# Neighbourhood heads first, the latent queries' and keys' units laid among them

## What is computed

```python
p = h @ w_in
q_lat, kv_lat, k_rope, na_qkv = split(p)
q = rmsnorm((rmsnorm(q_lat, q_norm) @ w_q_up).reshape(B, L, 8, 96), q_gain)
ckv = rmsnorm(kv_lat, kv_norm)
k_nope, v = split((ckv @ w_kv_up).reshape(B, L, 8, 128), [64])
k = rmsnorm(concatenate([k_nope, k_rope]), k_gain)
nq, nk = rmsnorm(na_q, na_q_gain), rmsnorm(na_k, na_k_gain)      # 8 neighbourhood (NA) heads of 64
```

## Time and profile before

| | us |
|---|---|
| median of 3 runs | 1404.86 (1399.4 to 1412.47) |
| the profiled execution's own time | 1393.2 |
| its span | 1391.4 |
| TensorE busy in the span | 1243.8 (89%) |
| VectorE busy | 605.8 (44%) |
| ScalarE busy | 272.8 (20%) |
| GpSimd busy | 201.1 (14%) |

### The profile page before, as it was taken

How to read it: one execution, slowest core, us unless ns; L and a number is a source line. 1 busy time by engine, 2 the same in 40 slices (tenths; PEclk the granted TensorE clock), 3 DMA queues, 4 the chain that set the end, 5 groups by cost and what they waited for, 6 DMA issues and landing times.

```text
span 1391.4 us, 26446 instructions
## 1 busy us (share of the span) xinstructions
PE 1243.8 (89%) x9235; PEld 720.8 (52%) x9236; DVE 605.8 (44%) x1303; ACT 272.8 (20%) x672; POOL 201.1 (14%) x249
## 2 busy tenths in 40 slices
PE   4899759989977899999989999999995989999996
PEld 3544435555454555555556565344545544555553
DVE  0221543435244244444454433578644243445445
ACT  1111323323020111121223212221001111222111
POOL 1021240000010022222210000111001022221231
PEclk9899968989977999999999999999995999999998
DMA  9542177776253199999993131100028059996794
GB/s 316 197 170 81 48 254 272 246 259 226 82 230 133 45 411 402 380 419 384 394 343 127 70 92 60 61 0 0 1 82 362 1 233 419 411 389 271 295 420 175
DMA packets 80145, 304.79 MB, mean 219 GB/s; under 512 B 10872, under 2 KB 11809, under 8 KB 54729
## 3 DMA queue, kind: packets, MB, share of 16 engines
q1 hardware_dynamic: 77098, 298.66, 55.5%
q10 hardware_dynamic: 2752, 4.53, 0.9%
q0 software_dynamic: 224, 0.61, 0.1%
HBM read 301.52 MB, written 2.24 MB: 218 GB/s over the span
## 4 chain that ended last, share of the span: by engine, by line
PE 83%; DVE 9%; issue 3%; DMA 1%; SPq 1%; ACT 1%; POOL 1%; POOLq 0%; DVEq 0%; ACTq 0%
PE banks L427 80%; DVE arena L949 4%; DMA arena<-in_ada_b 1%; DVE arena L1085 1%; PE banks L591 1%; SPq L1816 1%; ACT arena L1541 1%; POOL arena L1717 1%; PE banks L478 1%; DVE arena L1172 0%; DVE arena L1095 0%; SPq L1814 0%; PE banks L790 0%; DVE arena L1083 0%; DVE arena L960 0%
## 5 line engine op out<-in xcount | busy, mean ns | idle before, releaser
L427 PE MATMUL banks<-arena 32*128 32x256 f32 (+12 forms) x8904 | 1196.7, 425 | 78.0 <-DVE arena L949 15.6
L427 PEld LDWEIGHTS banks<-arena 128*32 128x32 f32 (+5 forms) x8904 | 679.3, 157 | 559.5 <-issue 405.5
L949 DVE TENSOR_TENSOR arena<-banks,arena 128x64 f32<-128x64 f32 (+4 forms) x284 | 113.9, 413 | 104.1 <-PE banks L427 69.7
L949 DVE TENSOR_TENSOR arena<-arena 128x384 f32<-128x384 f32 (+11 forms) x229 | 156.5, 689 | 4.5
L1205 DVE SCALAR_TENSOR_TENSOR arena<-arena 128x768 f32<-128x768 f32 x81 | 83.0, 1024 | 92.7 <-issue 88.5
L1742 POOL COPY arena<-arena 128x256 f32 x79 | 64.9, 822 | 289.3 <-PE banks L427 154.1
L1578 ACT ACTIVATE arena<-banks 128x512 f32<-128x512 f32 x79 | 47.2, 597 | 249.5 <-PE banks L427 249.5
L1215 DVE TENSOR_SCALAR arena<-arena 128x64 f32<-128x64 f32 x79 | 15.4, 195 | 174.9 <-ACT arena L1582 174.9
L1733 POOL TENSOR_TENSOR arena<-arena 128x256 f32<-128x256 f32 x81 | 59.6, 736 | 220.8 <-PE banks L427 220.8
L1716 POOL TENSOR_SCALAR arena<-arena 128x8 f32<-128x8 f32 (+2 forms) x28 | 10.4, 370 | 423.8 <-ACT arena L1438 297.6
L1304 DVE TENSOR_SCALAR arena<-arena 128x385 f32<-128x385 f32 x24 | 11.5, 481 | 82.4 <-ACT arena L1639 82.4
(11 more groups left out here) (144 smaller groups left out, 453.7 us busy)
## 6 DMA issues: line engine op xcount, KB each, us to landing
arena<-in_moe_w_gate SPq DMA_DIRECT2D x64, 1024.0 KB, 8.3
arena<-in_moe_w_up SPq DMA_DIRECT2D x64, 1024.0 KB, 10.4
arena<-in_moe_w_down SPq DMA_DIRECT2D x64, 1024.0 KB, 10.3
arena<-in_ada_w SPq DMA_DIRECT2D x24, 2048.0 KB
arena<-in_hy_w_in SPq DMA_DIRECT2D x6, 2048.0 KB
arena<-in_attn_w_in SPq DMA_DIRECT2D x3, 2048.0 KB
arena<-mod_rows SPq DMA_DIRECT2D x8, 512.0 KB, 10.2
arena<-in_attn_w_out SPq DMA_DIRECT2D x2, 2048.0 KB
```

The lines of the kernel that those rows point to most:

```text
L427: return pe.matmul(out, lhsT, rhs, start=start, stop=stop, skip_group_check=True)
L949: return dve.tensor_tensor(o, p, q, op)
```

## The change

The latent units go out of the block ahead of the heads; only the six NA units stay there. The heads' order is NA first. The seven latent units, in the order q 0, k 0 to k 3, q 1, q 2, are laid among the first 28 passes: unit b is produced in pass 4b, squared in 4b+1, reduced and raised to its power in 4b+2, normalised, turned and copied in 4b+3. The reduction and the normalising stand at the head of VectorE's pass. All 20 chunks are laid behind heads, one every 2.35 passes. The up-projection weights leave the ring and lie in room of their own (in the place of hT and of the gate rows), loaded behind chunk (0,6) and after the last NA value projection; the gate rows are loaded later. The bias is masked after the sixth power. PSUM banks are named: units 0 and 1, scores 2 and 3, transposed probabilities 4 and 5, head outputs 6, chunks and their columns 7.

```diff
+        wq = [v(HTO, NH * QK), v(HTO + NH * QK, NH * QK), v(MODO + 4 * D, NH * QK)]
+        wkv = v(MODO + 4 * D + NH * QK, NH * 2 * NOPE)
-        items0 = ([("ada", 0, n) for n in range(4)] + [("win", i) for i in range(4)] + [("up",)]
+        items0 = ([("ada", 0, n) for n in range(4)] + [("win", i) for i in range(4)]
...
-                 + [("q", t) for t in range(3)] + [("k", t) for t in range(4)])
+                 + [("q", 0)] + [("k", t) for t in range(4)] + [("q", 1), ("q", 2)])
...
-        at_unit = {7: chunks[0], 9: chunks[1]}
-        at_head = {int(2.6 * n) + 1: c for n, c in enumerate(chunks[2:])}
+        at_head = {int(2.35 * n) + 1: c for n, c in enumerate(chunks)}
-        heads = [(kind, t, hd) for kind in range(2) for t in range(T) for hd in range(NH)]
+        heads = [(kind, t, hd) for kind in (1, 0) for t in range(T) for hd in range(NH)]
+        def unit_stage(i, c):
+            b = (i - c) // 4
+            return 6 + b if (i - c) % 4 == 0 and 0 <= b < len(units) - 6 else None
...
@@ TensorE, produce and the heads
+                    pe.wait_ge(up_loaded, 64)
                     sig("latT").at(pe, t)
-                            o = open_(pe, "proj", i, [("normed", n)])
+                            o = open_(pe, "proj", i, [("normed", n)], j)
...
+                    if kind == 0 and hd == 0:
+                        sig("uT").at(pe, max(uT["q", t, 1], uT["k", 0 if t == 0 else 3, 1]))
-                    o = open_(pe, "S", i, [("expd", i)])
+                    o = open_(pe, "S", i, [("expd", i)], 2 + i % 2)
-                    o = open_(pe, "PT", i, [("PT", i)])
+                    o = open_(pe, "PT", i, [("PT", i)], 4 + i % 2)
-                        open_(pe, "O", i // 2, [("OT", i // 2)])
+                        open_(pe, "O", i // 2, [("OT", i // 2)], 6)
...
                     if i >= 2:
                         values(i - 2)
+                    if unit_stage(i, 0):
+                        produce(*units[unit_stage(i, 0)])
+                    if unit_stage(i, 3):
+                        turn_unit(*units[unit_stage(i, 3)])
                     if i in at_head:
-                        ada(*at_head[i])
+                        ada(*at_head[i], 7)
@@ VectorE (reduced and normalised are the two halves of the old unit loop)
+                for n in range(6):
+                    reduced(n)
+                    normalised(n)
                 for i in range(NU + 2):
+                    if unit_stage(i, 2):
+                        reduced(unit_stage(i, 2))
+                    if unit_stage(i, 3):
+                        normalised(unit_stage(i, 3))
                     if 1 <= i <= NU:
@@ ScalarE, behind the exponential
+                    if unit_stage(i, 1):
+                        square_unit(unit_stage(i, 1))
+                    if unit_stage(i, 3):
+                        turned(*units[unit_stage(i, 3)])
                     if i >= 2 and i % 2 == 1:
@@ GpSimd
+                for n in range(6):
+                    unit_power(n)
                 pool.wait_ge(in_bias, 16)
...
+                for n in range(6, len(units)):
+                    unit_power(n)
@@ SyncE
-                load(items0[8])
                 sp.dma_start(bias.rearrange("p a b c d -> p (a b c d)"), a["bias"]).then_inc(in_bias, 16)
-                for k in items0[9:]:
+                for k in items0[8:]:
                     load(k)
+                    if k == ("ada", 0, 6):
+                        sig("psum_proj").at(sp, proj["nv", T - 1, 0])
+                        for c in range(3):
+                            sp.dma_start(wq[c], a["mla_w_q_up"][0, c * P:(c + 1) * P, :]).then_inc(up_loaded, 16)
+                        sp.dma_start(wkv, a["mla_w_kv_up"][0]).then_inc(up_loaded, 16)
...
-                        if items[n][1:] == (0, 5):
+                        if items[n][1:] == (1, 5):
+                            sig("psum_proj").at(sp, proj["q", 2, 1])
                             load_gate(0, 0)
```

More of the change, by code:

```diff
@@ L285, in build @@
         number = {k: n for n, k in enumerate(items)}
-        ndma = {"ada": 2, "up": 2, "w3": 3}
+        ndma = {"ada": 2, "w3": 3}
         loads = [0, 0, 0]
@@ L337, in build @@
         n = 0
-        for kind, t in units + [("ck", 3)]:
+        for kind, t in units[:6] + [("ck", 3)] + units[6:]:
             for j in range(2 if kind in "qk" else 1):
@@ L557, in attention @@
                 produce("nq", 0)
[L558 to L565, removed]
-                        produce(*units[n + 1])
-                    if n in at_unit:
-                        ada(*at_unit[n])
+                for n, (kind, t) in enumerate(units[:6]):
+                    if n < 5:
+                        produce(*units[n + 1])
+                    else:
+                        for tt in range(T):
+                            produce("nv", tt)
+                        pe.wait_ge(in_ctx, 48)
+                        for tt in range(4):
+                            turn_latents(tt)
                     turn_unit(kind, t)
@@ L1019, in attention, with reduced @@
                     sig("lat").by(dve.tensor_copy(lat[:, t, QR + KVR:WIN0], kv[:, KVR:KVR + ROPE]), t)
[L1020 to L1023, removed]
+                def reduced(n):
+                    kind, t = units[n]
                     b = n % 2
@@ L1032, in attention, with normalised @@
                     sig("hms").by(red, n)
+                def normalised(n):
+                    kind, t = units[n]
+                    b = n % 2
                     sig("hrs").at(dve, n)
@@ L1044, in attention @@
                         sig("normed").by(tt(dv, dv, bc(nqg if kind == "nq" else nkg, NH, 1), ALU.mult), n)
-                        continue
+                        return
                     dv = d.rearrange("p (h w) -> p h w", h=NH)
@@ L1504, in attention @@
                 square_unit(0)
[L1505 to L1515 removed]
+                for n, (kind, t) in enumerate(units[:6]):
+                    if n < 5:
+                        square_unit(n + 1)
+                    else:
+                        for tt_ in range(T):
+                            o = read(act, "proj", proj["nv", tt_, 0])
+                            sig("nv").by(act.activation(V[:, tt_, NAW:], o, ACT.Copy), tt_)
+                        for tt_ in range(4):
+                            o = read(act, "latT", tt_).rearrange("p (c t) -> p c t", c=4)
+                            c0 = 0 if tt_ < T else 3
+                            sig("latT").by(act.activation(LT[:, c0:4, tt_ * P:(tt_ + 1) * P], o[:, c0:4, :], ACT.Copy), tt_)
                     turned(kind, t)
@@ L1780, in _, with unit_power @@
                     power(lat_rs[:, t, 0:2], lat_ms[:, t, 0:2], 2, "lat_rs", t)
-                for n in range(len(units)):
+                def unit_power(n):
                     sig("hms").at(pool, n)
                     power(hrs[:, n % 2, :], hms[:, n % 2, :], 8, "hrs", n)
+                for n in range(6):
+                    unit_power(n)
                 pool.wait_ge(in_bias, 16)
```

26 lines of the change are left out of this document (5 added, 21 removed).

## The result

The changed kernel takes 1417.73 us (median of 9, 1411.81 to 1420.24) against 1399.12 us of the kernel before, now a median of 9 (1394.26 to 1412.47). The ratio is 1.0135, 95% interval 1.0104 to 1.0165: 1.35% slower. The forecast was 0.7% slower and the range held the time. The forecast time, 1414.4 us, looks closer than it was: it was laid on a median of 1404.86, and the longer series moved that median down to 1399.12. The difference is 18.6 us, twice the 9.5 of the forecast and close to the +19.3 of the rival "the clock falls among the latent-tile heads". Of all runs in this document only three of units_mixed fell in a slower state of the chip; its median and ratio are given without them.

The account below looks back on a forecast made before the run. Heads were taken as chains filled by VectorE and ScalarE. Mark 47: 155.1 + 153.1 + 4.3 + 45.2 + 4 = 361.7 against 352.2, 9.5 us later; laid on the median, 1414.4 us, range 1404 to 1425, with rivals 1396 to 1430.

Parts of the forecast that it names:

- the clock falls among the latent-tile heads: Rival, 20%: sixteen heads and seven chunks at the lower clock, 13.8 us less the 4 charged; +19.3 us, 1424.
- The masking: Before the heads: masking the bias beside the value projections costs nothing and gains 5.4 us of contention.
- The stall: Before the first latent query: TensorE waits about 8.5 us for up-projection weights landing at 148.5, plus 2 us at lower clock.
- The units among the heads: Among the heads: seven latent units add 45.2 us, or 6.5 us each, what a unit costs alone.
- second rival: The rival "the clock stays up".
- a normalising: On VectorE ahead of the next reciprocal, all that follows waits: 20.5 us for seven, from 13 to 24.
- Reducing, 0.95 us in an idle of 0.74: 0.2 each: In head passes on VectorE: each unit's reduction mostly fits the wait for ScalarE's exponential; 1.4 us in all.
- The clock: Inside the heads: about five normalising pauses of TensorE lower the granted clock; 4 us charged (0 to 14).
- Turning the order of the two head kinds changes none of the 48 passes: Between marks 0 and 47: neighbourhood heads first costs nothing, so the old 153.1 us stay.
- The units hide: Rival, 15%: the heads have more room, so the 20.5 us of normalising go under waits; -11 us, 1394.
- the clock stays up: Rival, 12%: denser work gives back about 11 us the old heads lost to the clock; -7.5 us, 1397.
- no stall: Rival, 13%: weights arrive before TensorE asks, or the standing time is used; -1 us, 1404.

Follow-up runs that it names:

- units_mixed: Kernel before with early masking, weights loaded behind the bias, chunks behind seven units, and head pairs alternating between tiles: 1387.94 us, ratio 0.9929.
- fill_early: up_early with extra, unread matmuls in the passes with a normalising: 1386.41 us, ratio 0.9901 to the kernel before.
- mask_early: Kernel before with only the bias masking moved, after the sixth power instead of the last: 1390.14 us, ratio 0.9938.
- up_early: Changed kernel with up-projection weights loaded behind the bias and latent units ordered q 0 to q 2, k 0 to k 3: 1405.03 us, ratio 1.0106.
- fill_both: Changed kernel with extra, unread matmuls in the wait for the weights and in passes with a normalising: 1407.56 us, ratio 1.0059.
- fill_gaps: Changed kernel with extra, unread matmuls only in passes with a normalising, none in the wait for the weights: 1400.13 us, ratio 1.0009.
- na_first: mask_early with the neighbourhood heads first, all units still ahead of the heads: 1393.14 us, ratio 0.9997 to the kernel before.

## Why the prediction was right, and where it was short

**What bounds it.** Right. The heads had no room. With stall and pauses taken out (fill_early), the interleaved order reaches mark 47 at 211.7 us from the transposes and the separate one (mask_early) at 209.9.

**The masking.** Right, with its cover. The last unit's products take 5.4 us less in mask_early, and mark 0 comes 6.0 us earlier. In the changed kernel the collision stands at 118.06, where a product takes 3.15 us, and TensorE does not wait for it.

**The stall.** The mechanism was right, the cold start was right, and the size was 2 us short. Landing was predicted for 148.5 and came at 149.0, but that agreement is luck: the chunk's load was predicted to be issued at 136.26 and was issued at 134.81, so the weights took 14.2 us and not 12.2. TensorE asked 4.0 us behind the start of the transposes (138.6 and 134.62), as predicted (140 and 136.06). So it stood 10.4 us and not 8.5. For the lower clock behind the stall 2 us were added, and 2.2 were measured. From the transposes mark 0 was predicted at 19.0 us and came at 21.4. up_early confirms the price by taking it away: 12.7 us at mark 0.

**The units among the heads.** 45.2 us were predicted. What fill_both leaves for them, 202.2 - 153.1 - 4.3 = 44.8 us, looks like a confirmation and is none. The 153.1 us of the old heads contain about 11 us at the lower clock, by the prediction's own second rival, and fill_both gives most of such time back. The lengths of the passes, from mark to mark in ScalarE's timeline, show the terms. I take for each pass the shortest of the changed kernel, fill_both and fill_gaps, and subtract a plain pass (1.63 us at a prompt head, 2.45 at a latent tile, 2.1 to 2.2 more with a chunk). A plain pass at a latent tile lies between 2.40 and 2.56 us, so the sums are estimates, good to about 1 us:

| seven passes with | the sum had, us | measured, us |
|---|---|---|
| a produce | 14.4 | 14.6 |
| a reduction, squares and copies | 1.4 + 2.0 | 8.4 |
| a normalising | 20.5 | 23.3 |
| a turn | 6.9 | 6.4 |
| all | 45.2 | 52.7 |

Produces and turns were right. "Reducing, 0.95 us in an idle of 0.74: 0.2 each" was wrong: these passes are 0.5 to 1.9 us longer, because that idle is also where ScalarE does the squares, and the reduction waits for them (1.28 us in pass 14) before it takes its own 0.9. The 23.3 us are an upper value, since three of these seven passes are at a clock of 0.57 to 0.87 even in the shortest trace. What they hold too much, the clock below holds too little.

**The clock.** "I charge 4 us (0 to 14)" named the right cause and was somewhat short. The stretch grew by 64.0 us where the sum had 53.5. Less the two chunks and the 52.7 us of the table, 7.0 us are left for the clock. That is a net figure: the first 27 passes of the changed kernel are about 19 us longer than plain passes and the table together make them (155.1 against 83.3 + 52.7), while the old heads had lost about 11. fill_both takes 14.9 us back and fill_gaps 12.6. The clock falls behind each of the seven normalisings, not only behind five: the passes after them stand at 0.50 to 0.83. It does come back between some of them, to 1.00 in passes 4 and 5, 16 and 17, 20 and 21, 24 and 25. From 156 to 320 us the changed kernel spends 2 x (0.27 x 44 + 0.30 x 40 + 0.09 x 40 + 0.21 x 40) = 72 us at 1.2 GHz, fill_both 17. So the forecast was 12.9 us short at mark 47 (238.5 us from the transposes, where it had 225.6): 2.4 by the stall, 7.5 by the units and 3.0 by the clock. The rival priced at +19.3 us hit the difference but not by its own mechanism, which asked for 13.8 us by the clock. The range held the time; it is narrower than its terms' bounds added up (1392 to 1437), so it took the misses not to come all at once.

**The order of the heads.** "Turning the order of the two head kinds changes none of the 48 passes" is in doubt by some 4 us (na_first). If the order costs that, the clock's share in the changed kernel contains it.

**The other rivals.** "The units hide", "the clock stays up" and "no stall" fell with the first trace.

## What to carry to other kernels

A software pipeline like this one, whose period is a chain of short results, has no room to hide work in, however idle an engine looks in the busy shares: work laid into it added its full length on each engine in turn. Compare the wait that stands in one period with the piece to be laid in, and count a wait once: here squares on ScalarE and the reduction on VectorE were both laid into the same idle of VectorE. Put filler work where one engine waits long for another, as a chunk behind each unit did here (11.7 us off the heads' stretch for 3.9 us in the units'), and load the weights of moved work before it is asked for. On TensorE count pauses twice, once as idle time and once for the clock behind them.

## What was not expected of the hardware

Work that nobody reads made the kernel faster: 28 extra matmuls of 512 columns, 14.9 us less between the marks (217.1 to 202.2). The lower clock lasted into passes in which TensorE was busy without a break. In the changed kernel TensorE is busy throughout from 184.0 to 188.4 us at a clock of 0.50. Then one run of 80 records (values, a produced key unit, a chunk, the next scores) takes 8.09 us, at 0.50 in its first 4.0 us and 0.80 in the rest. In fill_both the same run takes 5.42 us at 1.00.

```profile
188.80 8.09 PE L435 MATMUL banks<-arena 128*64 128x128 f32 x80
```

```profile
182.68 5.42 PE L435 MATMUL banks<-arena 128*64 128x128 f32 x80
```
